# Neighbourhood attention in a hybrid backbone layer: the next tile's context scores before or behind the last tile's weighing

## The reference, cut to what matters

```
s_loc = einsum('brnqhd,brnlhd->brnhql', qb, kg) * scale + bias      # window
s_ctx = einsum('brnqhd,bphd->brnhqp', qb, k_ctx) * scale            # 512 context keys
p = softmax(concatenate([s_loc, s_ctx], axis=-1), axis=-1)
o = einsum(..., p[..., :L], vg) + einsum(..., p[..., L:], v_ctx)
```

## Time and profile before

| | |
|---|---|
| median of 3 runs | 2648.23 us (2647.66 to 2648.55) |
| the profiled execution | 2649.5 us, its span 2647.5 us, mean granted clock 0.987 |
| PE busy in the span | 2551.9 us (96%), 17663 matmuls |
| DVE, ACT, POOL busy | 1758.7 us (66%), 1289.4 us (49%), 266.5 us (10%) |
| attention, tiles 0 to 39 | about 391 to 607 us of the span |

### The profile page before, as it was taken

How to read it: one execution, slowest core, us unless ns; L and a number is a source line. 1 busy time by engine, 2 the same in 40 slices (tenths; PEclk the granted TensorE clock), 3 DMA queues, 4 the chain that set the end, 5 groups by cost and what they waited for, 6 DMA issues and landing times.

```text
span 2647.5 us, 41575 instructions
## 1 busy us (share of the span) xinstructions
PE 2551.9 (96%) x17663; PEld 1944.2 (73%) x17663; DVE 1758.7 (66%) x2082; ACT 1289.4 (49%) x1757; POOL 266.5 (10%) x226
## 2 busy tenths in 40 slices
PE   5999999999999999599999999999999999999997
PEld 4888876667878888477777777777777777777775
DVE  5699946775343444867766767667776776677767
ACT  5211245554232322445556555565555555555566
POOL 0112012220000000201011101101100110110110
PEclk9999999999999999799999999999999999999998
DMA  8531233202333742679788889979988988897995
GB/s 273 159 96 33 73 93 68 42 25 73 97 94 96 215 142 82 211 262 293 270 287 284 279 280 298 276 268 298 297 261 284 293 278 281 279 297 265 298 309 210
DMA packets 472290, 550.66 MB, mean 208 GB/s; under 512 B 30302, under 2 KB 424139, under 8 KB 472106
## 3 DMA queue, kind: packets, MB, share of 16 engines
q1 hardware_dynamic: 464330, 526.36, 61.5%
q0 software_dynamic: 7776, 21.63, 3.6%
HBM read 518.58 MB, written 29.38 MB: 207 GB/s over the span
## 4 chain that ended last, share of the span: by engine, by line
PE 93%; DVE 2%; SPq 1%; ACT 1%; DMA 1%; issue 1%; POOL 0%; DVEq 0%; ACTq 0%; POOLq 0%
PE bank L790 88%; PE bank L793 5%; SPq L454 1%; DMA arena<-in_w_ada 0%; DVE slot_lo L2329 0%; ACT arena L1502 0%; DVE arena L2347 0%; DMA arena<-in_cache_ctx_k 0%; DMA arena<-in_w_attn_o 0%; DVE arena L2038 0%; DVE arena L2045 0%; DVE lo_first L2325 0%; DVE arena L2237 0%; DVE arena L2236 0%; DMA yacc<-arena 0%
## 5 line engine op out<-in xcount | busy, mean ns | idle before, releaser
L2325 DVE TENSOR_TENSOR slot_lo<-slot,e_hi 128x2048 fp32r<-128x2048 f32 x254 | 574.7, 2289 | 161.1 <-ACT e_hi L1722 156.5
L1722 ACT ACTIVATE e_hi<-slot 128x2048 fp32r<-128x2048 f32 x256 | 480.6, 1914 | 24.8 <-PE bank L790 24.8
L790 PE MATMUL bank<-e_hi,xe_hi 128*128 128x512 f32 x1024 | 419.1, 409 | 6.0 <-DVE xe_lo L2413 6.0
L790 PE MATMUL bank<-e_hi,xe_lo 128*128 128x512 f32 x1024 | 405.4, 396 | 0.0
L790 PE MATMUL bank<-slot_lo,xe_hi 128*128 128x512 f32 x1016 | 397.4, 391 | 0.0
L790 PE MATMUL bank<-slot,arena 128*32 128x256 f32 x6144 | 351.2, 380 | 0.0
L790 PE MATMUL bank<-arena 128*64 128x128 f32 (+8 forms) x2470 | 330.4, 362 | 21.1 <-ACT arena L1502 6.4
L2329 DVE TENSOR_TENSOR slot_lo<-slot,e_hi 128x2048 fp32r<-128x2048 f32 x128 | 288.9, 2289 | 76.6 <-ACT e_hi L1724 76.6
L790 PEld LDWEIGHTS bank<-arena 128*64 128x64 f32 (+3 forms) x2470 | 223.8, 155 | 100.8 <-issue 49.4
L790 PEld LDWEIGHTS bank<-slot,arena 128*32 128x32 f32 x6144 | 189.9, 110 | 137.5 <-issue 22.0
L1724 ACT ACTIVATE e_hi<-slot 128x2048 fp32r<-128x2048 f32 x128 | 239.4, 1912 | 28.1 <-PE bank L790 28.1
(11 more groups left out here) (269 smaller groups left out, 3602.5 us busy)
## 6 DMA issues: line engine op xcount, KB each, us to landing
slot<-in_w_gate_e SPq DMA_DIRECT2D x128, 1024.0 KB, 5.9
slot<-in_w_up_e SPq DMA_DIRECT2D x128, 1024.0 KB, 9.1
slot<-in_w_down_e SPq DMA_DIRECT2D x128, 1024.0 KB, 7.0
arena<-in_w_in SPq DMA_DIRECT2D x68, 512.0 KB, 5.2
arena<-in_w_ada SPq DMA_DIRECT2D x48, 512.0 KB, 7.0
arena<-in_w_conv_pw SPq DMA_DIRECT2D x24, 256.0 KB, 5.7
arena<-in_w_attn_o SPq DMA_DIRECT2D x24, 256.0 KB, 5.3
yacc<-arena SPq DMA_DIRECT2D x10, 512.0 KB, 2.6
```

What stands on the lines that cost most here:

```text
L790: return nc.tensor.matmul(out, lhsT, rhs, start=start, stop=stop)
L1722: A_(halves(e_hi[c % 2])[:, :, rows4, :], halves(slot[q])[:, :, rows4, :], ACT.Copy).then_inc(ehi_ok, 1)
L2325: V_.tensor_tensor(halves(lo)[:, :, rows4, :], halves(slot[q])[:, :, rows4, :], halves(e_hi[c % 2])[:, :, rows4, :].bitcast(F32), ALU.subt ...
```

## The change

In the loop over g on PE the two lines that issue `scores_context(g + 1)` are moved from behind `weigh(g - 1)` to ahead of it. The instructions, their operands, their semaphores and the streams of all other engines stay as they are.

```
                 if g + 1 < NP and LOC[g + 1]:
                     scores_local(g + 1)
+                if g + 1 < NP:
+                    scores_context(g + 1)
                 if g:
                     weigh(g - 1)
-                if g + 1 < NP:
-                    scores_context(g + 1)
```

## The result

The changed kernel takes 2695.06 us (median of 4 runs, 2693.98 to 2695.79), the kernel before 2648.39 us in the same comparison: a ratio of 1.0175, with a 95% interval of 1.0163 to 1.0187. The forecast was 2688.6 us in 2671 to 2703, slower. The profiled execution has a span of 2692.0 us, 44.5 more than before.

A forecast was written before the change was run, and what follows sets the result against it. PE was taken to bound the kernel, at 5.49 us per latent tile; the longer steps summed to 8.74 + 21.58 + 10.02 = +40.3 us, giving 2688.6 us on the median's scale, range 2671 to 2703 for 8 in 10.

The forecast's parts named there:

- The ring: Loop through PE's scores and weighing, DVE's multiplication and maxima, ACT's exponentials: 6.75 us per latent tile against 5.49; 82%.
- latent, i = 1 to 6: Six steps of a head pair between latent tiles, each 6.75 us from one negated maximum to the next, together 40.50.
- i = 7: Step from tile 7 of a head pair to the next, with a prompt tile's scores and a full weighing: 5.77 us.
- i = 8: Step from tile 8 to the next, with a prompt tile's scores and shorter wait for them: 5.34 us.
- i = 9: Step from tile 9 to the next head pair, with a prompt tile's weighing costed at 0.60: 5.13 us.
- i = 0: Step from a head pair's tile 0 to the next, with a prompt tile's weighing costed at 0.60: 5.56 us.
- recorded signs: Trace signs in attention: period near 6.75 us, PE idle about 1.2 before the scores, PE busy near 204 of some 257.
- the clock is costed at nothing: TensorE's granted clock in attention was to stay 1.00, with latent tiles 81% busy and idle times of about 1.26 us.
- The rival of a falling clock: In every second latent step TensorE runs at 1.2 GHz, adding 51 us: about 2739 us; chance 5%.
- PE's wait alone: DVE is not held; only PE's 0.98 us wait in 24 latent steps counts: +23.5, 2672 us; chance 6%.
- No change: ACT releases the scores' banks in time at 474.59, so PE keeps its period of 5.49: 2648 us; chance 4%.
- faster: At head pairs' ends, earlier scores let the weighing fill PE's idle time, at most 12.67 us: 2636 us; chance 3%.

The follow-up runs named there:

- x4: The changed kernel with the context scores issued in the middle of the weighing, DVE and ACT as they were: 2670.02 us, ratio 1.0084 to the kernel before.
- y1: The changed kernel with 12 unused transposes ahead of the context scores in the steps i = 0 and i = 7: 2687.19 us, ratio 1.0148 to before.
- x1: The changed kernel; DVE takes both maxima before multiplying tile g-2, ACT the context exponentials before its copy: 2636.57 us, again 2636.83 (0.9961, 0.9956 to before).
- y3: The changed kernel with both of DVE's maxima ahead of CA's copy, multiplication and ACT unchanged: 2671.77 us, ratio 1.0091 to the kernel before.
- y4: The changed kernel run again without edits, for comparison and a second trace: 2694.77 us, ratio 1.0180 to the kernel before.
- z2: The changed kernel with ACT's context exponentials ahead of its copy of CB, DVE as it was: 2695.45 us, ratio 1.0182 to the kernel before.

## Why the prediction was right, and by how much it was off

**The ring, step by step.** The steps from one negated maximum to the next (L2065) in the trace after:

| step | forecast | measured |
|---|---|---|
| latent, i = 1 to 6 | 6.75 | 6.73 |
| i = 7 | 5.77 | 5.77 (444.00 to 449.77) |
| i = 8 | 5.34 | 5.34 (449.77 to 455.11) |
| i = 9 | 5.13 | 5.22 (455.11 to 460.33) |
| i = 0 | 5.56 | 5.63 (460.33 to 465.96) |
| tile 1 to tile 10 | 56.74 | 56.71 (403.62 to 460.33) |

The terms hold: PE waits ahead of the scores, DVE 2.51 us ahead of the multiplication, released by the engines that were named. Two of the recorded signs did not come: PE's row shows 0.92 us of idle time ahead of the scores and not 1.2, and PE is busy 216 us in attention and not near 204. PE's rows cover 5.81 us of a step of 6.73, where the work was 5.49. The weight loads resolve it. They pause 0.23 us ahead of R (478.86), whose bank the copy of CA frees (478.11 + 0.68). The scores' loads start at 481.12, where they would have come at 480.12: the last loads end at 479.58, and 0.54 is the usual pause. So 5.49 us of work, 1.00 of wait and 0.23 ahead of R make 6.72. The short waits are hidden inside PE's rows, some 8 us over 24 steps; the rest of the 12 us fits the work at half clock. The steps i = 9 and i = 0 are longer by the prompt tile's weighing, costed at 0.60 by its matmuls alone; as x4 shows, a short burst has a fixed part. One reading was loose: the 28 "matmuls" of a weighing are 28 records of 14 matmuls (8 of 4 for a prompt tile). The durations were taken per record, so no number changes.

**The term that was mis-sized** is "the clock is costed at nothing". From tile 1 to tile 39 (403.62 to 648.16) it took 244.54 us, where the forecast had 198.17 + 40.34 = 238.51; the 6.0 us are in the stretches where the clock fell (63.93 us from tile 10 to 20, 65.37 from 20 to 30, 58.53 from 30 to 39, for 62.30, 62.30 and 57.17), and y1, whose clock doesn't fall, has 62.33 and 62.32 us for the two whole pairs. I had compared the busy share and the idle time of a latent step with the stretch at a pair's end before, and not worked out PE's idle time in the other steps: at i = 7 PE has no window scores to compute ahead of the wait, and at i = 0 a prompt tile's short transposes lie ahead of it, so its idle time is 1.7 us, longer than the 1.41 that I had compared with, and than the 1.59 at the first tile, the longest in attention before. A comparison of lengths would not have settled it, though: in x4 the clock falls behind 1.33 us. The reading that the trace before shows falls "only where idleness is far longer" was wrong too. That trace has one at the end of attention, among idle times of at most 0.82 us:

```profile
604.00:608.00 4.00, 3.20 (x16) 0.64 0.01 4
```

The rival of a falling clock was right in kind and wrong in place (every second latent step) and price (51 us; it cost 6 to 8). The Trainium skill ("TensorE: Matmul & The Clock Gate", section "HAM oscillation — how this bites in real kernels") tells of the same kind of loss: idle stretches between bursts of matmuls send the clock down. y1 agrees in kind, with 7.6 us. But the page speaks of longer waits, for DMAs, and here waits of 1.70 to 1.77 us for another engine were enough.

**The span** adds up: +46.4 from tile 1 to 39, -0.6 since the first context maximum came earlier in this trace (403.62 for 404.26), -1.2 behind tile 39: +44.5. The medians are 46.7 apart, as single executions differ by 1 to 2 us.

**The rivals.** PE's wait alone (2672) is out by the steps, by x1, where it would have stayed, less clearly by x4, and by y3: in y3 DVE is less in the way, and the wait for the scores is gone while another takes its place. No change and faster are out too. PE's order itself saves 0.20 us a tile, which only x1 lets through. This is not the mechanism of the faster rival (idle time at the pairs' ends), and its bound of 12.67 us of idle time does not cover it, since it shortens what the earlier trace rows count as busy. The forecast had taken the 5.49 us as PE's fixed work.

## What to carry to other kernels

Before an instruction is moved on one engine, follow the ring through the orders of all engines: here 0.98 us of a wait on PE held the weighing, the weighing held DVE's maxima, and these the wait itself, so the tile cost 1.24 us more. The orders of engines belong together: each of the two orders of PE was the best with one order of DVE and ACT and cost 47 us with the other. And before the clock is taken as constant, TensorE's idle times are to be worked out for every kind of step, not only for the common one: here they cost 6 to 8 us at seven places between the latent steps. Their length alone does not tell where the clock will fall.

## What the runs showed of the hardware

- Behind idle times of TensorE of 1.70 to 1.77 us the granted clock fell to half for some us: four times of seven in one trace, three of seven in y4, five of seven in z2. The 24 idle times of 0.92 us, once in each step of 6.73, left it at 1.00.
- The length of the single idle time does not decide alone. The clock fell behind all three of 1.33 us in x4, but behind none of the three of 1.34 and 1.35 in x1, and before the change behind neither those of 1.41 and 1.42 nor the one of 1.59. What tells these apart, no run shows.
- The weight loads pause for 0.76 us behind the context scores (whether transposes or a weighing follow) and 0.17 behind a weighing (whether transposes or context scores follow); why, no run shows. Putting the two kinds of scores side by side saved 0.20 us of 5.49 a tile; cutting a weighing in two cost 0.36 (2 x 1.02 for 1.68).
